# The output product of two chunks as seven block products, formed with Strassen's scheme, in a one-core layer kernel

## The chip, the cores and the metric

The kernel runs on one core of a Trainium2 chip. The metric is the device time of one execution in microseconds (us). The engines are TensorE (PE in the profile, its weight loads PEld), VectorE (DVE), ScalarE (ACT), GpSimd (POOL) and SyncE (SP), which here issues every DMA. Each has its own instruction stream and executes it in order; semaphores join them.

## What is computed

The reference, cut to the part that matters here (one layer, 2048 tokens, 1024 channels, float32):

```python
shift, scale, gate = jnp.split(jax.nn.silu(c) @ w_ada + b_ada, 3, axis=-1)
h = _layer_norm(x) * (1 + scale[:, None]) + shift[:, None]
xa, ga, u, v, gb = jnp.split(h @ w_in, SPLITS, axis=-1)          # 5 x 512 channels
ya = _pool_mixer(xa, w_pool, pool_scale) * jax.nn.silu(ga)
yb = _sgu_mixer(gelu(u), gelu(v), ...) * jax.nn.silu(gb)
y = jnp.concatenate([ya, yb], axis=-1) @ w_out                   # (2048,1024) @ (1024,1024)
z = DEEPNORM_ALPHA * x + gate[:, None] * y
return _layer_norm(z) * ln_g + ln_b
```

## The kernel before

The 2048 tokens are worked in four chunks of T = 512. Every product runs three times in float32r: both factors are split into a high part (ScalarE rounds, `wH`, `hH`, `yH`) and a low part (VectorE subtracts, `wL`, `hL`, `yL`), and `product` (L1050) issues high by high, high by low and low by high.

A chunk consists of units, each with one 128x1024 block of weights (512 KB). Units 0 to 3 (`V_UNITS`) make v in banks A, token by token. Units 4 to 19 are the channel units, four for each of the groups g = 0..3 (xa, ga, u, gb), in banks B 0 to 3. Units 20 to 27 are the output units: four make the first 512 columns of y @ w_out in banks A, four the second in banks B. A unit is 24 matmuls of 512 columns. Chunk 0 has a start of its own, chunks 1 and 2 are a loop (`run_chunks`, L230), and chunk 3 has its own end (`last_products`).

Weights pass through two float slots, `wF`. SP loads unit n+4 in its iteration n (`load_w`, L305) once the low part of unit n+2 is made; ScalarE copies unit n+2 in its iteration n (`split_high`, L511) into one of four slots once unit n-2 is done on TensorE; VectorE makes the low part (`split_low`, L658). The order of each engine's work within an iteration is written out by hand; tables say in which iteration a piece stands.

Pieces beside the units: `pooling`, `gate` and `y_pool` make the pooling branch of a group in `yP`, `sgu_sum`, `mix` and a multiplication by the gate the other branch in `mixed`; `y_low` makes the low parts. The next chunk's x is prepared meanwhile: statistics by tokens in iterations 10, 11, 14, 15 (`X_STATS_IN`); in iteration 16 SP sends means and reciprocal deviations through DRAM and loads x by channels; `x_normalise` (two VectorE instructions of 512 columns for each of eight rows) stands in iterations 19 to 22 (`X_CENTRE_IN`); `h_evacuate` on ScalarE and `h_split` on VectorE in 20 to 23.

After an output half, `z_half` (L892) multiplies the bank by the gate, adds it to ALPHA * x in `z` and takes statistics; the second half's are made in iterations 0 to 3 of the next chunk, with `z_norm` behind them. GpSimd makes the reciprocal deviations (`rstd`, L459: a power on one or four elements) in the order in which its stream holds them: z of the last chunk, v, x of the next. TensorE may start a chunk's v units when z's first-half products have read banks A.

## Time and profile before

| | |
|---|---|
| time, median of 3 | 673.99 us (673.91 to 674.61) |
| profiled execution | 673.68 us |
| its span, first to last instruction | 671.6 us |
| busy: TensorE, VectorE, ScalarE, GpSimd | 659.8, 516.1, 235.1, 61.7 us |
| mean granted TensorE clock | 0.998 of full speed |
| moved by DMA | 108.73 MB, 162 GB/s |

Busy times are sums over instructions; those of TensorE overlap each other, so a row's mean is longer than the distance from one matmul to the next. The chain is followed back from the last instruction and shows which engine set the end. Idle time in front of an instruction is written behind it with what ended it.

### The profile page before, as it was taken

The page shows a single profiled execution, that of the slowest core. Times are in us where ns is not written, and L with a number is a line of the kernel's source. Part 1 is how long each engine was busy: PE and PEld are TensorE (multiplying, and loading weights), DVE is VectorE, ACT ScalarE, POOL GpSimd, SP SyncE. Part 2 cuts the span into 40 slices and gives each one's busy share as a digit, 9 for nine tenths or more (in the row PEclk, how much of TensorE's full clock was granted, in tenths as well). Part 3 has the DMA queues.
Part 4 walks back from the last instruction along what each step waited for, and adds up shares of the span by engine and source line. Part 5 has one row for each costly group of instructions (what it writes and reads, how often), then busy time and mean ns, then how long its engine had stood idle before and what let it go on. Part 6 is the DMA issues. An engine that isn't in the chain of part 4 may idle for free.

```text
span 671.6 us, 8845 instructions
## 1 busy us (share of the span) xinstructions
PE 659.8 (98%) x3103; PEld 551.3 (82%) x3103; DVE 516.1 (77%) x956; ACT 235.1 (35%) x307; POOL 61.7 (9%) x77
## 2 busy tenths in 40 slices
PE   8999999999999999999999999999999999999995
PEld 8888888877888888888888888888888888888884
DVE  5678898749969967766979968775977986656776
ACT  4424644316522333224722332322821333323300
POOL 2000110100002201100002201000002210000010
PEclk9999999999999999999999999999999999999999
DMA  8995643785334472288243562378343454224111
GB/s 340 365 332 233 219 153 116 163 228 189 125 111 141 126 258 86 95 116 322 96 156 100 180 248 65 106 94 332 102 148 90 162 205 159 104 79 154 52 63 62
DMA packets 34546, 108.73 MB, mean 162 GB/s; under 512 B 6573, under 2 KB 7633, under 8 KB 34514
## 3 DMA queue, kind: packets, MB, share of 16 engines
q1 hardware_dynamic: 34514, 108.31, 49.5%
q8 instruction: 19, 0.31, 0.2%
q14 instruction: 13, 0.11, 0.1%
HBM read 97.80 MB, written 10.50 MB: 161 GB/s over the span
## 4 chain that ended last, share of the span: by engine, by line
PE 95%; issue 2%; DVE 2%; ACT 0%; DMA 0%; POOLq 0%; POOL 0%; DVEq 0%
PE bank_b L1053 63%; PE bank_a L1053 25%; PE bank_a L1180 2%; PE bank_a L1140 1%; PE bank_b L1113 1%; PE bank_a L1171 1%; DVE w_low L656 1%; PE bank_b L1077 0%; DVE v_gelu L708 0%; PE bank_b L1171 0%; PE bank_b L1132 0%; PE bank_b L1104 0%; DMA vector_rows<-in_vectors 0%; ACT h_high L528 0%; ACT w_high L509 0%
## 5 line engine op out<-in xcount | busy, mean ns | idle before, releaser
L1053 PE MATMUL bank_b<-h_high,w_high 128*128 128x512 f32 x512 | 202.2, 395 | 0.2 <-DVE h_low L668 0.2
L1053 PE MATMUL bank_b<-h_low,w_high 128*128 128x512 f32 x512 | 199.3, 389 | 0.0
L1053 PE MATMUL bank_b<-h_high,w_low 128*128 128x512 f32 x512 | 199.3, 389 | 0.0
L661 DVE TENSOR_TENSOR w_low<-w_float,w_high 128x1024 fp32r<-128x1024 f32 x98 | 119.5, 1220 | 40.3 <-ACT w_high L518 40.2
L518 ACT ACTIVATE w_high<-w_float 128x1024 fp32r<-128x1024 f32 x98 | 103.4, 1056 | 130.5 <-DMA w_float<-in_w_units 57.2
L1053 PEld LDWEIGHTS bank_b<-h_high,w_high 128*128 128x128 f32 x512 | 96.2, 188 | 20.2 <-issue 1.1
L1053 PEld LDWEIGHTS bank_b<-h_high,w_low 128*128 128x128 f32 x512 | 96.1, 188 | 20.1
L1053 PEld LDWEIGHTS bank_b<-h_low,w_high 128*128 128x128 f32 x512 | 96.2, 188 | 19.5 <-issue 0.5
L461 POOL TENSOR_TENSOR z_rstd<-z_var_eps,minus_half 128x1 f32<-128x1 f32 x16 | 22.0, 1377 | 361.8 <-DVE z_var_eps L905 351.9
L1053 PE MATMUL bank_a<-w_high,y_high 128*128 128x512 f32 x128 | 49.9, 390 | 0.2 <-issue 0.2
L1053 PE MATMUL bank_a<-w_high,y_low 128*128 128x512 f32 x128 | 49.8, 389 | 0.0
L1053 PE MATMUL bank_a<-w_low,y_high 128*128 128x512 f32 x128 | 49.8, 389 | 0.0
L1053 PE MATMUL bank_b<-w_high,y_high 128*128 128x512 f32 x96 | 37.3, 389 | 0.0
L1053 PE MATMUL bank_b<-w_low,y_high 128*128 128x512 f32 x96 | 37.3, 389 | 0.0
L1053 PE MATMUL bank_b<-w_high,y_low 128*128 128x512 f32 x96 | 37.3, 389 | 0.0
L1053 PE MATMUL bank_a<-w_high,h_high 128*128 128x512 f32 x96 | 37.3, 389 | 0.0
L1053 PE MATMUL bank_a<-w_low,h_high 128*128 128x512 f32 x96 | 37.3, 389 | 0.0
L1053 PE MATMUL bank_a<-w_high,h_low 128*128 128x512 f32 x96 | 37.3, 389 | 0.0
L461 POOL TENSOR_TENSOR x_rstd<-x_var_eps,minus_half 128x1 f32<-128x1 f32 x16 | 20.1, 1255 | 138.8 <-DVE x_var_eps L684 138.8
L611 ACT ACTIVATE tanh<-bank_b 128x512 f32<-128x512 f32 x15 | 9.0, 598 | 60.8 <-PE bank_b L1053 60.8
L1053 PEld LDWEIGHTS bank_a<-w_high,y_high 128*128 128x128 f32 x128 | 24.0, 188 | 5.6 <-issue 0.6
L1053 PEld LDWEIGHTS bank_a<-w_high,y_low 128*128 128x128 f32 x128 | 24.0, 188 | 5.0
(180 smaller groups left out, 934.0 us busy)
## 6 DMA issues: line engine op xcount, KB each, us to landing
w_float<-in_w_units SPq DMA_DIRECT2D x90, 512.0 KB, 3.4
x_norm<-in_x SPq DMA_DIRECT2D x16, 512.0 KB, 4.5
z<-in_x SPq DMA_DIRECT2D x16, 512.0 KB, 5.2
out<-z SPq DMA_DIRECT2D x15, 512.0 KB, 4.8
z<-in_mod_units SPq DMA_DIRECT2D x12, 512.0 KB, 9.1
x_norm<-in_x_channels SPq DMA_DIRECT2D x12, 512.0 KB, 15.0
w_float<-xa_units SPq DMA_DIRECT2D x12, 512.0 KB, 3.5
mod_spare<-in_mod_units SPq DMA_DIRECT2D x6, 512.0 KB, 8.6
```

The source lines that it names most:

```text
L461: nc.gpsimd.tensor_tensor(rstd_out, var_eps, exponent, ALU.pow).then_inc(ready, 1)
L518: nc.scalar.activation(wH[:, n % S_SLOTS, :], w_float(c, n), ACT.Copy).then_inc(w_high, 1)
L611: nc.scalar.activation(tanh[:, :], B[:, 1, :], ACT.Tanh, scale=0.5).then_inc(ga_tanh, 1)
L656: vec.tensor_tensor(low, early_float(unit), high.bitcast(F32), ALU.subtract).then_inc(w_low, 1)
L661: vec.tensor_tensor(wL[:, n % S_SLOTS, :], w_float(c, n), wH[:, n % S_SLOTS, :].bitcast(F32), ALU.subtract).then_inc(w_low, 1)
L1053: last = mm(bank, wl if n == 2 else wh, ml if n == 1 else mh, start=start and n == 0, stop=stop and n == 2)
L1113: last = mm(B[:, 3, at:at + P], m_slot(m)[:, col:col + P], c_col.broadcast_to([P, P]), start=(m % 2 == 0 and a == 0 and s == 0), stop=(m = ...
L1140: mm(A[:, 0, 0:P], ident[:, :], ones[:, :], start=True, stop=True)
L1171: last = mm(banks[k // 4][:, k % 4 * P:(k % 4 + 1) * P], xa_float(g)[:, cut], wpF[:, g * P:(g + 1) * P], start=True, stop=True)
L1180: last = mm(A[:, 2 + h % 2, j * P:(j + 1) * P], gv[:, j, cut], wt[:, cut], start=True, stop=True)
```

## The change

Chunks 1 and 2 (`FAST`) make the output product as a 2 x 2 block product in the Winograd form of Strassen's scheme: y is cut by tokens (256 and 256) and by branch (pooling and SGU), the weights by branch and by output half. Seven block products take the place of eight; each is two units of 12 matmuls, so such a chunk has 14 output units. The gate is multiplied into the weights beforehand.

- In chunk 0, from the moment the gate is known, GpSimd forms the seven weight blocks for each quarter q of the input channels (`prepare_out_units`), SP loads the weights for it in iterations 18, 19, 24, 26 and stores the seven half-units (256 KB each) to DRAM in iterations 23, 25, 27 and in iteration 1 of chunk 1. Chunk 1's v activation waits for all of the stores, since the last tiles lie in `gv`.
- In the fast chunks GpSimd forms the sums of y for each group (`sums_of_y`); ScalarE and VectorE split two of them at once and two in iterations 25 to 28.
- VectorE adds each product's banks to z as it is finished (`add_parts`); products 4 to 6 reuse banks B.
- The preparation of the next x moves in the fast chunks: statistics to iterations 8 to 11, rows to 12, centring to 16 to 19, h to 22 to 32.
- The loop over chunks 1 and 2 is unrolled; unit counts go through `base(c)`.

The core of the diff:

```diff
+FAST = (1, 2)
+PRODUCTS = 7
+FAST_UNITS = IN_UNITS + 2 * PRODUCTS
+PARTS = ((0, 0, 0, 0), (0, 1, 1, 0), (1, 2, 2, 0), (1, 3, 3, 0), (2, 4, 0, 0), (2, 5, 1, 0), (3, 6, 2, 1), (3, 7, 3, 1),
+         (4, 4, 0, 1), (4, 5, 1, 1), (5, 6, 0, 1), (5, 7, 1, 1), (6, 4, 2, 1), (6, 4, 2, 0), (6, 5, 3, 1), (6, 5, 3, 0))
+READ_IN = {IN_UNITS + 3 + 2 * i: i for i in range(PRODUCTS - 1)}
+LATE_IN = {25: 0, 26: 1, 27: 2, 28: 3}
...
+FAST_X_STATS_IN = {8: 0, 9: 1, 10: 2, 11: 3}
+FAST_X_ROWS_IN = 12
+FAST_X_CENTRE_IN = {16: (0, 1), 17: (2, 3), 18: (4, 5), 19: (6, 7)}
+FAST_H_IN = {22: (0,), 23: (1,), 24: (2,), 26: (3,), 28: (4,), 29: (5,), 30: (6,), 32: (7,)}
...
-            chunk(0, True, False)
-            with eng.Fori(1, CHUNKS - 1) as c:
-                chunk(c, False, False)
-            chunk(CHUNKS - 1, False, True)
+        def run_chunks(chunk):
+            for c in range(CHUNKS):
+                chunk(c, c == 0, c == CHUNKS - 1)
...
+            def prep_load(q):
+                if q == 0:
+                    sp.wait_ge(w_low, XA_ALONE[-1] + 1)
+                elif q == 1:
+                    sp.wait_ge(sgu_done, G)
+                else:
+                    sp.wait_ge(out_stored, (q - 1) * PRODUCTS * 16)
+                for half in range(2):
+                    sp.dma_start(prep_tile(q, half), w_units[IN_UNITS + half * G + q]).then_inc(prep_landed[q % 2][half], 16)
+            def prep_store(q):
+                sp.wait_ge(prep_ready, q + 1)
+                zero, one = prep_tile(q, 0), prep_tile(q, 1)
+                for i, half_unit in enumerate((zero[:, 0:T], t4[:, :], zero[:, T:], t12[:, 0:T], t12[:, T:], one[:, 0:T],
+                                               one[:, T:])):
+                    cut = slice(q % 2 * T, (q % 2 + 1) * T)
+                    sp.dma_start(out_units[i, q // 2][:, cut], half_unit).then_inc(out_stored, 16)
...
+            def prepare_out_units():
+                gp = nc.gpsimd
+                pool.wait_ge(gate_ready, 2)
+                for q in range(G):
...
+                        pool.wait_ge(prep_landed[q % 2][half], (q // 2 + 1) * 16)
+                        done = gp.tensor_tensor(rows, rows, gate.broadcast_to([P, 2, T]), ALU.mult)
+                    prep_steps.then(pool, done)
+                    b21, b11, b22, b12 = zero[:, 0:T], zero[:, T:], one[:, 0:T], one[:, T:]
+                    wait(pool, out_stored, q * PRODUCTS * 16)
+                    prep_steps.then(pool, gp.tensor_tensor(t12[:, 0:T], b12, b11, ALU.subtract))
+                    prep_steps.then(pool, gp.tensor_tensor(t12[:, T:], b22, t12[:, 0:T], ALU.subtract))
+                    gp.tensor_tensor(t4[:, :], b21, t12[:, T:], ALU.subtract)
+                    gp.tensor_tensor(b12, b22, b12, ALU.subtract).then_inc(prep_ready, 1)
+            def sums_of_y(c, g):
...
+                gp.tensor_tensor(s12[:, 0:half], a21, a22, ALU.add).then_inc(s_steps, 1)
+                pool.wait_ge(s_steps, nth + 1)
+                gp.tensor_tensor(s12[:, half:], s12[:, 0:half], a11, ALU.subtract).then_inc(s12_ready, 1)
+                gp.tensor_tensor(s34[:, g, 0:half], a11, a21, ALU.subtract)
+                pool.wait_ge(s12_ready, nth + 1)
+                gp.tensor_tensor(s34[:, g, half:], a12, s12[:, half:], ALU.subtract).then_inc(s34_ready, 1)
...
+                        if n == ys_in[g] and c in FAST:
+                            act.wait_ge(ys_ready, c * G + g + 1)
+                            nc.scalar.activation(aH[:, g, :], mixed[:, 0:T // 2], ACT.Copy)
+                            act.wait_ge(s12_ready, FAST.index(c) * G + g + 1)
+                            nc.scalar.activation(yH[:, G + g, :], s12, ACT.Copy).then_inc(ys_high, 1)
...
+            def add_parts(c, i):
+                nth = FAST.index(c) * len(PARTS)
+                dve.wait_ge(unit_done, base(c) + IN_UNITS + 2 * i + 2)
+                for p, (product, bank, j, half) in enumerate(PARTS):
...
+                    if earlier:
+                        dve.wait_ge(part_read, nth + earlier[0] + 1)
+                        ins = vec.tensor_tensor(z[:, j, cut], psum, z[:, j, cut], ALU.add)
+                    else:
+                        dve.wait_ge(z_landed[j], (c + 1) * 16)
+                        ins = vec.scalar_tensor_tensor(out=z[:, j, cut], in0=z[:, j, cut], scalar=ALPHA, in1=psum,
+                                                       op0=ALU.mult, op1=ALU.add)
+                    ins.then_inc(part_read, 1)
...
+            def fast_unit(c, w, i, r):
...
+                if r == 0 and i >= 4:
+                    pe.wait_ge(part_read, nth * len(PARTS) + 2 * i - 2)
+                bank0 = (0, 2, 4, 6, 4, 6, 4)[i]
+                for qq in range(2):
+                    q = 2 * r + qq
+                    if i == 0:
+                        pe.wait_ge(yp_low, c * G + q + 1)
+                    if i == 2:
+                        pe.wait_ge(ys_low, c * G + q + 1)
+                    if i == 5:
+                        pe.wait_ge(s34_low, nth * G + q + 1)
...
+                    for t in range(2):
+                        psum = (A, B)[bank0 // 4][:, bank0 % 4 + t, :]
+                        cut = slice(col + t * P, col + (t + 1) * P)
+                        done = product(psum, high[:, at, cut], low[:, at, cut], w[0][:, block], w[1][:, block],
+                                       start=(i < 4 and q == 0), stop=(q == G - 1), skip_group_check=(i > 3))
```

## Rows read from the trace of the kernel before

**Rows 1.** the page: busy per engine, its slices of DMA, the chain

```profile
PE 659.8 (98%) x3103; PEld 551.3 (82%) x3103; DVE 516.1 (77%) x956; ACT 235.1 (35%) x307; POOL 61.7 (9%) x77
...
GB/s 340 365 332 233 219 153 116 163 228 189 125 111 141 126 258 86 95 116 322 96 156 100 180 248 65 106 94 332 102 148 90 162 205 159 104 79 154 52 63 62
...
PE 95%; issue 2%; DVE 2%; ACT 0%; DMA 0%; POOLq 0%; POOL 0%; DVEq 0%
```

**Rows 2.** the chain in order of time, chunk 2: start, us, what

```profile
464.05 21.76 PE bank_a L1053 x96
```

**Rows 3.** windows: chunk 0's output units; chunk 1's v units, channel units

```profile
core 0: us, PE busy (x) PEld busy (x) DVE busy (x) ACT busy (x) POOL busy (x), PEclk, DMA share, GB/s
151.90:195.70 43.80, 43.80 (x193) 36.27 (x194) 36.05 (x49) 21.86 (x27) 0.00 (x0) 1.00 0.44 150
195.70:217.40 21.70, 21.70 (x97) 17.96 (x97) 21.00 (x34) 4.25 (x4) 6.20 (x4) 1.00 0.37 122
217.40:308.10 90.70, 90.70 (x418) 75.68 (x417) 64.50 (x143) 28.98 (x40) 10.11 (x8) 1.00 0.53 153
```

**Rows 4.** groups by shape: busy us, mean ns; idle before

```profile
L661 DVE TENSOR_TENSOR w_low<-w_float,w_high 128x1024 fp32r<-128x1024 f32 x98 | 119.5, 1220 | 40.3 <-ACT w_high L518 40.2
...
L668 DVE TENSOR_TENSOR h_low<-sum_a,h_high 128x512 fp32r<-128x512 f32 x16 | 11.0, 687 | 2.2 <-ACT sum_a L529 2.2
...
L897 DVE TENSOR_TENSOR tanh<-bank_a,gate_rows 128x512 f32<-128x512 f32 x15 | 10.3, 684 | 0.3 <-PE bank_a L1053 0.3
...
L1030 DVE SCALAR_TENSOR_TENSOR z<-z,tanh 128x256 f32<-128x256 f32 x2 | 0.9, 426 | 0.1
```

**Rows 5.** chunk 2's float slots: VectorE, ScalarE, DMA to landing

```profile
484.02 1.22 DVE L661 TENSOR_TENSOR w_low<-w_float,w_high 128x1024 fp32r<-128x1024 f32 x1
...
488.57 1.06 ACT L518 ACTIVATE w_high<-w_float 128x1024 fp32r<-128x1024 f32 x1 [1.14 <-DMA w_float<-in_w_units]
...
DMA to landing us min/median/max: 3.2/3.3/3.3
```

**Rows 6.** VectorE in order of time, chunk 2's iterations 16 to 19

```profile
442.92 0.69 DVE L975 TENSOR_TENSOR mixed<-mixed,gate_b 128x512 f32<-128x512 f32 x1
...
447.58 0.18 DVE L821 COPY xa<-xa_halo 128x16 f32<-128x16 f32 x1 [1.11 <-ACT xa L608]
...
451.43 1.22 DVE L661 TENSOR_TENSOR w_low<-w_float,w_high 128x1024 fp32r<-128x1024 f32 x1
...
454.43 0.74 DVE L865 SCALAR_TENSOR_TENSOR mixed<-bank_a,half_cols,sgu_bias 128x512 f32<-128x512 f32 x1
461.25 1.23 DVE L661 TENSOR_TENSOR w_low<-w_float,w_high 128x1024 fp32r<-128x1024 f32 x1 [6.07 <-ACT w_high L518]
...
463.59 0.68 DVE L689 TENSOR_TENSOR x_norm<-x_norm,x_mean_rows 128x512 f32<-128x512 f32 x1
...
464.92 0.69 DVE L689 TENSOR_TENSOR x_norm<-x_norm,x_mean_rows 128x512 f32<-128x512 f32 x1
```

**Rows 7.** GpSimd's selections, by shape

```profile
L478 POOL TENSOR_SCALAR_AFFINE_SELECT y_pool<-y_pool 128x512 f32<-128x512 f32 x1 | 1.0, 962 | 25.2 <-DMA y_pool<-in_w_sgu 25.2
...
L456 POOL TENSOR_SCALAR_AFFINE_SELECT identity<-identity 128x128 f32<-128x128 f32 x1 | 0.3, 292 | 0.0
```

**Rows 8.** GpSimd's powers in order of time, and VectorE beside one

```profile
198.37 1.50 POOL L461 TENSOR_TENSOR z_rstd<-z_var_eps,minus_half 128x1 f32<-128x1 f32 x1 [70.19 <-DVE z_var_eps L905]
...
223.45 1.04 POOL L461 TENSOR_TENSOR v_rstd<-v_var_eps,minus_half 128x4 f32<-128x4 f32 x1 [0.41 <-DVE v_var_eps L883]
...
639.01 0.56 POOL L461 TENSOR_TENSOR z_rstd<-z_var_eps,minus_half 128x1 f32<-128x1 f32 x1 [95.25 <-DVE z_var_eps L905]
...
198.24 1.23 DVE L661 TENSOR_TENSOR w_low<-w_float,w_high 128x1024 fp32r<-128x1024 f32 x1
```

**Rows 9.** VectorE at the end of chunk 0's output units

```profile
187.07 0.68 DVE L897 TENSOR_TENSOR tanh<-bank_a,gate_rows 128x512 f32<-128x512 f32 x1
...
195.71 0.69 DVE L897 TENSOR_TENSOR tanh<-bank_b,gate_rows 128x512 f32<-128x512 f32 x1 [3.02 <-PE bank_b L1053]
```

More of the change, by code:

```diff
@@ L228, in wait, with units, base, own @@
                 eng.wait_ge(s, value)
-        def run_chunks(eng, chunk):
-            chunk(0, True, False)
-            with eng.Fori(1, CHUNKS - 1) as c:
-                chunk(c, False, False)
-            chunk(CHUNKS - 1, False, True)
+        def run_chunks(chunk):
+            for c in range(CHUNKS):
+                chunk(c, c == 0, c == CHUNKS - 1)
+        def units(c):
+            return FAST_UNITS if c in FAST else UNITS
+        def base(c):
+            return sum(units(i) for i in range(c))
+        def own(c, n):
+            return (c, n) if n < units(c) else (c + 1, n - units(c))
+        def classic(c):
+            return sum(1 for i in range(c) if i not in FAST)
         def places(first):
@@ L376, in chunk @@
             def chunk(c, first, last):
-                for n in range(V_UNITS if first else 0, UNITS):
+                _, x_rows_in, _, _ = x_tables(c)
+                for n in range(V_UNITS if first else 0, units(c)):
                     if first and n == V_UNITS + 2:
@@ L407, in chunk @@
                         sp.dma_start(xn[:, j, :], x_tiles[c + 1, j]).then_inc(xn_landed[j], 16)
-                    if not last and n == 16:
+                    if not last and n == x_rows_in:
                         sp.wait_ge(x_rstd, (c + 2) * TILES)
@@ L419, in chunk @@
                                 .then_inc(xT_landed[i], 16)
-                    if not last and n == 17:
+                    if not last and n == x_rows_in + 1:
                         sp.wait_ge(rows_stored, (c + 1) * 32)
@@ L491, in chunk @@
                     rstd(v_rstd, vve[:, j, :], vrs[:, j, :], minus_half[:, :])
-                if not last:
+                if c in FAST:
+                    x_rstds(c + 1, 0)
+                    x_rstds(c + 1, 1)
+                    sums_of_y(c, 0)
+                    x_rstds(c + 1, 2)
+                    x_rstds(c + 1, 3)
+                    for g in range(1, G):
+                        sums_of_y(c, g)
+                elif not last:
                     for j in range(TILES):
                         x_rstds(c + 1, j)
-            run_chunks(pool, chunk)
+                if first:
+                    prepare_out_units()
+            run_chunks(chunk)
             for j in range(TILES):
@@ L591, in chunk @@
                 sgu_after, mix_in, ys_in = places(first)
-                for n in range(FIRST_LOOP if first else 0, IN_UNITS + 1 if last else UNITS):
+                _, _, _, h_in = x_tables(c)
+                for n in range(FIRST_LOOP if first else 0, IN_UNITS + 1 if last else units(c)):
                     if not (last and n in LAST_SPLITS_IN):
@@ L639, in chunk @@
                                 .then_inc(gate_ready, 1)
-                    if not last and IN_UNITS <= n < IN_UNITS + 4:
-                        for k in range(2 * (n - IN_UNITS), 2 * (n - IN_UNITS) + 2):
+                    if not last and n in h_in:
+                        for k in h_in[n]:
                             h_evacuate(c + 1, k)
-            run_chunks(act, chunk)
+            run_chunks(chunk)
         @block.vector
@@ L858, in sgu_sum @@
                 wait(dve, ys_low, c * G + g)
+                done = sum(1 for i in FAST if i < c) * G + (g if c in FAST else 0)
+                wait(dve, s34_ready, done)
                 if first and g == 0:
@@ L941, in chunk @@
                     first_branches(c)
-                for n in range(FIRST_LOOP if first else 0, IN_UNITS + 1 if last else UNITS):
+                x_stats_in, _, x_centre_in, h_in = x_tables(c)
+                for n in range(FIRST_LOOP if first else 0, IN_UNITS + 1 if last else units(c)):
+                    if c in FAST and n in READ_IN:
+                        add_parts(c, READ_IN[n])
                     if not (last and n in LAST_SPLITS_IN):
```

221 lines of the change are left out of this document (166 added, 55 removed).

## The prediction

> **What bounds the kernel now.** I read the page first: TensorE is busy 98% of the span and makes 95% of the chain that ended last [rows 1]. The reader is to see there that only fewer matmuls, or a stall of TensorE, can move the end. The chain in order of time gives the price: 96 matmuls of 512 columns take 21.76 us wherever they stand [rows 2], so 0.2267 us each (the 389 ns of a single row overlap the next one and are no price). A unit of 24 is 5.44 us, the eight output units of a chunk 43.5 us. Then the windows by stage show what else is full: VectorE is busy 36.1 of 43.8 us in chunk 0's output stage and 21.0 of 21.7 us in the four v units after it; only the channel units leave it room, 64.5 of 90.7 us [rows 3]. GpSimd does nothing but small powers. So TensorE bounds, VectorE is second and close, and everything that the change gives VectorE, or puts in its way, has to be laid against that.
>
> **Matmuls removed.** A fast chunk has 14 units of 12 matmuls, 168, where there were 192. 48 fewer in two chunks are 48 x 0.2267 = 10.9 us, all on the path. The ideal output stage is 168 x 0.2267 = 38.1 us, and a fast unit 2.72 us. Nothing is regained if the same stage waits for 5.4 us.
>
> **Work added per fast chunk.** Six more units to split: ScalarE 1.06 us, VectorE 1.14 us each (a 1220 ns row, of which 0.08 overlaps the next start). Sixteen half-tile additions from PSUM to z at 0.61 to 0.72 us take the place of eight gate products and eight additions: even. Four late high/low pairs of 0.6 us, four half-size ones of about 0.4 us (256 columns take 426 ns) [rows 4].
>
> **The two float slots.** Each weight unit must land, be copied and be split before its slot is loaded again. In chunk 2 the split that began at 484.02 ended at 485.24, the load issued behind it took 3.3 us, ScalarE copied at 488.57, VectorE could split from 489.65 to 490.87 [rows 5]. The ring is 3.3 + 1.06 + 1.22 + 0.07 = 5.65 us for two units; TensorE now asks for two in 5.44, where before it asked for two in 10.9. A ring that was half idle becomes the pace.
>
> **VectorE into the output stage, in before's clock of chunk 2.** The eight centrings move from iterations 19 to 22 into 16 to 19; each is 1.33 us [rows 6]. I lay the work end to end from 443.6, where the third SGU group's gated product ends: wait for GpSimd's two sums and ScalarE's copy 2.0 (GpSimd priced below, 0.55 each; before, the wait was 0.7), the two low parts 1.0, centring 2.66, split 1.14, pooling of the last group 3.85, centring 2.66, split 1.14, gate, product and sum 2.28, centring 2.66, split 1.14, mix and low part 1.20, centring 2.66, split 1.14, gate and product 1.47, the GpSimd wait again 2.0, low parts 1.0, split 1.14. That is 31.1 us and ends at 474.7 with the split of unit 23. The 6.07 us that VectorE idled before 461.25 are used up. TensorE wants unit 23 at 464.05 + 3 x 2.72 = 472.2: a stall of 2.5 us. The statistics of x that leave iterations 14 and 15 go into earlier idle time and cost nothing: those iterations begin with waits for ScalarE. If the cover fails, 2 us each come on top.
>
> From there the ring gives unit 33 five turns later, 474.7 + 28.25 = 503.0, and the stage ends at 505.7: 41.6 us. But VectorE serves the ring in order. Fourteen splits are 16.0 us, twelve PSUM additions, each pair behind a finished product, 8.0, eight low parts of h and four late ones 7.3: 31 of the 38 us. Adding the ring's waits where they fall, unit 28 (its bank is free only after product 2 was added in iteration 27) starts 2.5 us late, and units 27, 30 and 32 lose 0.1 to 0.6 each; that lay-out ends at 508.9, 44.8 us. Bounds are 38.1 and 44.8; between 41.6 and 44.8 I take 43.0, because the waits of additions and of the ring partly coincide. So a fast stage gains 0.5 us instead of 5.4, two gain 1.0. The v units after it get less VectorE work (no gate product; the first takes four additions), so they cost nothing; TensorE's banks B are asked for 22 us later.
>
> **GpSimd's preparation in chunk 0.** Before has no large two-input GpSimd instruction. The nearest are the selections: 128x128 in 0.29 us and 128x512 in 0.96, a slope of 1.74 ns per element with one input [rows 7]. Two inputs cost no less, and at most double, 3.5 ns; I take a quarter above the row, 2.2, nearer to the row. Per quarter of the weights it does two products of 1024 and four differences of 512, 4096 elements: 9.0 us; four are 36 us (28.5 and 57 at the bounds); a sum of 256 columns in the fast chunks is 0.55 us.
>
> Can it lie beside VectorE? The power on a single element tells. It takes 0.56 us at 639.01, and 1.50 at 198.37, begun beside a 1024-column difference of VectorE that ran to 199.47; so do 25 of its 32 rows on one element, at 1.46 to 1.59 us, all but the first four and the last few [rows 8]. Four elements beside VectorE's work on v, which reads one tensor, take 1.04 us at 223.45. So GpSimd waits out VectorE's instructions with two SBUF inputs. That the reverse holds no row shows; but whichever yields, the two are not abreast, and someone waits for each: GpSimd's products are waited for by SP's in-order stores (behind which the weight loads stand) and its z powers by VectorE. So I price them as one resource.
>
> The Trainium skill (SBUF — State Buffer, Who interferes with whom) says that a VectorE instruction with two SBUF inputs and a GpSimd instruction that reads SBUF exclude each other for the whole instruction. The rows above agree for GpSimd's side. Its GPSIMD Engine Reference, Performance versus the Vector engine, gives 4497 ns for a 2048-element tensor_tensor, so 36.0 us for the preparation, which would leave the sum as it is.
>
> It starts near 154: the gate is in SBUF at 151.8, the first loads go out near 147 behind a full DMA stretch. Nearly all that VectorE does from there to 187 has two SBUF inputs, save the z products, statistics and one gate. Its last product on banks A ends at 187.8 while the v units need them at 195.7: 8 us of room [rows 9]. With the round trip of each store (1.8 MB, about 6 us at the 340 GB/s that the page's fullest slices show [rows 1]) GpSimd does about 22 of its 36 us by then. 5 us of it fall on other VectorE work, 2 into idle time: 15 us late against 8 of room, TensorE stalls 7. The last 14 us meet a VectorE that is 97% full in the v units; 5 us of idle before them and about 4 us of overlap leave some 5 more of lateness, most of it inside the two-unit lead of the splits: 1 us. Sum 8 us; at 1.74 ns 3 to 4 us. At 3.5 ns it is 8 + 21 = 29 us. Below nothing it can't go, as nothing is taken out. ScalarE's v activation waits for the last store: done near 212, needed at 217.4; free, but a late GpSimd would show there.
>
> DMA: 4.2 MB loaded and 7.3 MB stored over some 65 us, 177 GB/s on 120 to 150 [rows 3]; each store holds a weight load up by some 5.5 us, but before the fast chunks the ring has 10.9 us a turn. Free there. Unrolling removes loop branches that the chain doesn't show: 0. Fewer matmuls, no change of the granted clock, 1.00 throughout.
>
> **Sum.** The terms come from the profiled execution, 673.68 us for a span of 671.6; the median of the runs is 0.3 us above it, 673.99. 673.7 - 1.0 + 8 = 680.7, and with the 0.3 us 681.0 us.
>
> **Rivals.** (a) *Preparation hidden, fast stage at the ring's pace.* GpSimd and VectorE run side by side, or the waiting falls on GpSimd alone in gaps. For it: only 1-element reads are seen to collide. Then stages of 40.6 to 41.6 us: 674.0 - 2 x 2.4 = 669.2. It decides for faster once the preparation costs under about 4 us with stages under 41.6. Chance 0.25. (b) *Preparation hidden, stage 43.0*: 673.0. Chance 0.15. (c) *Two inputs double GpSimd's element*: 674.0 - 1.0 + 29 = 702; 0.10. (d) *Full gain*: neither ring nor VectorE shows, 663 to 666; against it the ring row. 0.04. My forecast, 676 to 688, has 0.46.
>
> A measurement tells 0.2%, 1.3 us, from nothing. Faster: 0.25 of (a), 0.05 of (b), 0.04 of (d), 0.03 from the forecast's edge, 0.37. Same 0.08, mostly (b). Slower 0.55. The range 667 to 690 takes in (a), (b), the forecast and the lower bounds; it leaves (c) and (d), 0.14, outside, and the forecast's far edge.
>
> **What would show it.** In the profile after: 48 fewer 512-column matmuls in fast chunks; GpSimd's products near 2.3 us alone and longer beside splits; VectorE's splits in chunk 0's output stage above 1.22 us, or late; TensorE idle just before chunk 1's first v unit; in the fast chunks, output stages near 43 us with ScalarE's copies waiting for loads, and gaps ahead of units 23 and 28. I'm wrong if VectorE's rows keep 0.69 and 1.22 us beside GpSimd's large ones, or if the fast stages take under 41 us.

## The result, and the profile after

The changed kernel takes 715.18 us, median of four executions (714.60 to 717.07), beside 673.95 us for the kernel before on the same chip: a ratio of 1.0617, 95% interval 1.0594 to 1.0641. That is 41 us slower, where 7 us slower was forecast and 690 us was the top of the range.

The page of the changed kernel: busy times of two engines, granted TensorE clock by slices, the chain. It answers to [rows 1].

```profile
PE 666.6 (93%) x3055; PEld 548.3 (77%) x3055; DVE 555.0 (78%) x984; ACT 254.4 (36%) x335; POOL 128.3 (18%) x133
...
PEclk9999999998999999999899999999899999999998
...
PE 37%; DVE 30%; DMA 13%; issue 9%; POOL 5%; ACT 4%; SPq 1%; POOLq 0%; DVEq 0%; ACTq 0%
```

TensorE has its 48 matmuls fewer (3055 for 3103), yet its busy time is longer, and the chain, 95% TensorE before, is TensorE for 37% only, with VectorE, DMA and GpSimd for 48%. VectorE's busy time rose by 39 us, though it has only 28 more instructions (12 of them are splits of weights, `w_low`, of 1.22 us). Windows by stage, for [rows 3]: chunk 0's output units, chunk 1's v, channel and output units, chunk 2's output units.

```profile
152.10:207.46 55.36, 45.50 (x193) 36.93 (x193) 47.09 (x47) 20.79 (x26) 29.28 (x14) 0.94 0.60 217
207.46:230.91 23.45, 22.02 (x97) 17.92 (x97) 15.62 (x20) 4.25 (x4) 18.44 (x12) 1.00 0.73 262
230.91:333.74 102.83, 94.39 (x416) 76.28 (x416) 80.12 (x168) 30.78 (x44) 21.59 (x22) 0.98 0.54 159
333.74:385.96 52.22, 44.39 (x168) 34.12 (x169) 42.77 (x55) 29.59 (x38) 2.85 (x4) 0.90 0.53 176
498.89:551.13 52.24, 43.08 (x168) 33.27 (x169) 42.64 (x55) 29.99 (x38) 2.85 (x4) 0.93 0.54 177
```

The first column after the window is the stage's length. Against before (43.8, 21.7, 90.7 and 43.5 us) the first three grew by 11.6, 1.7 and 12.1 us, and each fast output stage by 8.7 us. There are two separate losses: one from chunk 0's output units on, where GpSimd prepares the weights, and one in each fast stage.

**The first loss.** VectorE in order of time, in chunk 0's output units:

```profile
154.45 2.76 DVE L839 TENSOR_TENSOR x_norm<-x_norm,x_rstd_rows 128x512 f32<-128x512 f32 x1
157.14 3.42 DVE L810 TENSOR_TENSOR w_low<-w_float,w_high 128x1024 fp32r<-128x1024 f32 x1
160.48 0.68 DVE L993 SCALAR_TENSOR_TENSOR gate_b<-tanh,bank_b 128x512 f32<-128x512 f32 x1
...
170.19 2.71 DVE L839 TENSOR_TENSOR x_norm<-x_norm,x_rstd_rows 128x512 f32<-128x512 f32 x1
...
174.03 1.21 DVE L810 TENSOR_TENSOR w_low<-w_float,w_high 128x1024 fp32r<-128x1024 f32 x1
```

and GpSimd beside it, with the row after its long wait:

```profile
154.16 5.31 POOL L582 TENSOR_TENSOR mod_spare<-mod_spare,gate_rows 128x1024 f32<-128x1024 f32 x2 [25.69 <-DMA mod_spare<-in_w_units]
159.55 2.15 POOL L586 TENSOR_TENSOR w_spare<-mod_spare 128x512 f32<-128x512 f32 x1
...
166.76 5.58 POOL L582 TENSOR_TENSOR v_gelu<-v_gelu,gate_rows 128x1024 f32<-128x1024 f32 x2
194.19 1.29 POOL L586 TENSOR_TENSOR w_spare<-v_gelu 128x512 f32<-128x512 f32 x1 [21.84 <-DMA out_units<-mod_spare]
...
200.97 4.71 POOL L582 TENSOR_TENSOR mod_spare<-mod_spare,gate_rows 128x1024 f32<-128x1024 f32 x2
```

A normalisation of 0.69 us takes 2.76 us, a split of 1.22 us takes 3.42 us. The pair of GpSimd products ends at 159.47 and the split 1.09 us later: it stands still until the product is done and then takes about its own time. The row at 160.48 reads one tensor from a bank and keeps its 0.68 us beside a GpSimd difference. As GpSimd stops at 172.3, the split is back at 1.21 us. GpSimd itself takes 1.29 us for a difference of 512 when it is alone and 2.15 us beside VectorE. The split at 174.03 is unit 23's. In the kernel before the same split is this row:

```profile
162.62 1.22 DVE L661 TENSOR_TENSOR w_low<-w_float,w_high 128x1024 fp32r<-128x1024 f32 x1
```

There it ended 4.4 us ahead of TensorE's need (at 162.62 + 1.22, needed at 151.90 + 3 x 5.44). In the changed kernel TensorE stands from 168.70 for it, 6.59 us, and this is what the granted clock does (windows of 2 us, PEclk is the third number from the end):

```profile
166.00:168.00 2.00, 2.00 (x10) 1.65 (x10) 2.00 (x2) 0.69 (x1) 2.00 (x2) 1.00 0.00 0
...
172.00:174.00 2.00, 0.00 (x0) 0.00 (x0) 2.00 (x3) 0.38 (x1) 0.35 (x1) 0.50 0.00 0
174.00:176.00 2.00, 0.71 (x2) 0.61 (x3) 1.97 (x4) 2.00 (x4) 0.00 (x0) 0.50 0.00 0
176.00:178.00 2.00, 2.00 (x6) 1.54 (x5) 1.97 (x4) 1.49 (x2) 0.00 (x0) 0.50 0.80 260
178.00:180.00 2.00, 2.00 (x10) 1.63 (x9) 2.00 (x3) 1.39 (x2) 0.00 (x0) 0.94 0.02 6
```

In the stall it falls from 1.00 to 0.50 (from 2.4 to 1.2 GHz) and it is back only after some 3 us of work, in which the same matmuls take twice as long: 6 of them between 176 and 178, 10 in a window at full clock.

SP in order of time: it comes to the first store at 185.63, to the last group of stores at 226.60, and the weight load that is queued behind those goes out at 230.88. So ScalarE, in the second fence, starts a copy for the channel units late:

```profile
185.63 0.43 SPq L400 DMA_DIRECT2D out_units<-mod_spare  x1
...
226.60 0.32 SPq L400 DMA_DIRECT2D out_units<-v_gelu  x1
...
230.88 0.33 SPq L375 DMA_DIRECT2D w_float<-in_w_units  x1
```

```profile
237.23 1.06 ACT L652 ACTIVATE w_high<-w_float 128x1024 fp32r<-128x1024 f32 x1 [11.40 <-DMA w_float<-in_w_units]
```

VectorE waits for GpSimd directly as well. The powers of z stand in GpSimd's stream behind the last quarter of the weights, so VectorE idles 5.15 us for them, and the split that follows at 229.63 is the one for which TensorE waits 1.43 us at the start of the channel units:

```profile
226.53 1.07 POOL L547 TENSOR_TENSOR z_rstd<-z_var_eps,minus_half 128x1 f32<-128x1 f32 x2
```

```profile
227.11 1.28 DVE L1099 SCALAR_TENSOR_TENSOR z<-z,z_mean_var,ln_g_rows 128x1024 f32<-128x1024 f32 x1 [5.15 <-POOL z_rstd L547]
```

**The second loss.** VectorE ahead of and in chunk 2's output stage, which begins at 498.89:

```profile
477.78 1.23 DVE L810 TENSOR_TENSOR w_low<-w_float,w_high 128x1024 fp32r<-128x1024 f32 x1 [9.23 <-ACT w_high L652]
...
482.83 0.69 DVE L1177 TENSOR_TENSOR mixed<-mixed,gate_b 128x512 f32<-128x512 f32 x1
485.84 0.98 DVE L1031 TENSOR_TENSOR ys_low<-mixed,ys_high 128x256 fp32r<-128x256 f32 x1 [2.32 <-ACT y_high L768]
...
503.63 1.22 DVE L810 TENSOR_TENSOR w_low<-w_float,w_high 128x1024 fp32r<-128x1024 f32 x1
...
508.62 1.22 DVE L810 TENSOR_TENSOR w_low<-w_float,w_high 128x1024 fp32r<-128x1024 f32 x1
...
515.05 2.35 DVE L810 TENSOR_TENSOR w_low<-w_float,w_high 128x1024 fp32r<-128x1024 f32 x2
```

The splits at 503.63, 508.62 and 515.05 are those of units 21, 22 and 23. TensorE waits for the first and the third, and later for a bank that `add_parts` reads (unit 28):

```profile
504.90 0.50 PE L1257 MATMUL bank_a<-w_high,y_high 128*128 128x512 f32 x1 [2.96 <-DVE w_low L810]
...
516.31 0.79 PE L1257 MATMUL bank_a<-w_high,y_high 128*128 128x512 f32 x1 [3.41 <-DVE w_low L810]
...
533.80 0.47 PE L1257 MATMUL bank_b<-w_high,y_high 128*128 128x512 f32 x1 [1.89 <-DVE z L1051]
```

With one of 0.52 us these gaps are 8.8 us. The stage is 52.24 us and its matmuls are 38.1. Of the other 5.3 us some 3.3 are matmuls at half clock, behind the two long gaps (TensorE's busy time times what the granted clock lacks of 1.00, summed over 50 windows of the stage); the rest is in gaps below 0.4 us and in the start behind each gap, where the first two matmuls stand 0.34 us apart and not 0.23.

The 9.23 us ahead of 477.78 are a wait for a weight load that SP issued behind the four loads of the next x by channels. It was issued at 462.80, and ScalarE copied its weights at 476.68:

```profile
457.75 1.93 SPq L504 DMA_DIRECT2D x_norm<-in_x_channels  x4
462.80 0.33 SPq L375 DMA_DIRECT2D w_float<-in_w_units  x1
```

The kernel before has the same pair four iterations later, and its 6.07 us ahead of 461.25 [rows 6] are the wait for it:

```profile
442.37 2.02 SPq L418 DMA_DIRECT2D x_norm<-in_x_channels  x4
446.51 0.34 SPq L316 DMA_DIRECT2D w_float<-in_w_units  x1
```

### The profile page after: what moved, and what is told of

The parts are those of the page before. It is cut to its first block, busy times and chain, and to the rows that moved or that the text cites. A ratio compares the mean times of both kernels' runs of the same rounds, so it can differ in the third digit from the quotient of the medians.

```text
span 715.3 us, 8443 instructions
## 1 busy us (share of the span) xinstructions
PE 666.6 (93%) x3055; PEld 548.3 (77%) x3055; DVE 555.0 (78%) x984; ACT 254.4 (36%) x335; POOL 128.3 (18%) x133
## 3 DMA queue, kind: packets, MB, share of 16 engines
q1 hardware_dynamic: 41426, 126.14, 53.7%
## 4 chain that ended last, share of the span: by engine, by line
PE 37%; DVE 30%; DMA 13%; issue 9%; POOL 5%; ACT 4%; SPq 1%; POOLq 0%; DVEq 0%; ACTq 0%
PE bank_b L1257 24%; DMA w_float<-in_w_units 8%; PE bank_a L1257 8%; DVE w_low L810 7%; DMA w_float<-out_units 3%; DVE x_norm L837 3%; DVE z L1101 1%; ACT w_high L652 1%; DVE z L1099 1%; SPq L400 1%; DVE x_stats L830 1%; DVE y_low L1033 1%; PE bank_a L1344 1%; DMA out_units<-mod_spare 1%; DVE mixed L1177 1%
## 5 line engine op out<-in xcount | busy, mean ns | idle before, releaser
L810 DVE TENSOR_TENSOR w_low<-w_float,w_high 128x1024 fp32r<-128x1024 f32 x110 | 139.6, 1271 | 58.3 <-ACT w_high L652 58.2
L652 ACT ACTIVATE w_high<-w_float 128x1024 fp32r<-128x1024 f32 x110 | 115.9, 1056 | 184.8 <-DMA w_float<-in_w_units 131.2
L1257 PEld LDWEIGHTS bank_b<-h_high,w_high 128*128 128x128 f32 x512 | 96.5, 189 | 31.1 <-DVE w_low L810 11.0
L1257 PEld LDWEIGHTS bank_b<-h_high,w_low 128*128 128x128 f32 x512 | 96.5, 189 | 20.3
L1257 PE MATMUL bank_a<-w_high,y_high 128*128 128x512 f32 x96 | 42.1, 438 | 21.3 <-DVE w_low L810 21.1
L547 POOL TENSOR_TENSOR z_rstd<-z_var_eps,minus_half 128x1 f32<-128x1 f32 x16 | 19.8, 1239 | 234.7 <-DVE z_var_eps L1094 117.2
L1257 PEld LDWEIGHTS bank_a<-w_high,y_high 128*128 128x128 f32 x96 | 19.8, 206 | 30.1 <-DVE w_low L810 25.5
L1257 PE MATMUL bank_a<-w_low,y_high 128*128 128x512 f32 x96 | 40.9, 426 | 0.0
L1257 PE MATMUL bank_a<-w_high,y_low 128*128 128x512 f32 x96 | 40.8, 425 | 0.0
L547 POOL TENSOR_TENSOR v_rstd<-v_var_eps,minus_half 128x4 f32<-128x4 f32 x16 | 16.4, 1024 | 78.8 <-DVE v_var_eps L1072 78.8
L1257 PEld LDWEIGHTS bank_b<-w_high,y_high 128*128 128x128 f32 x96 | 18.0, 188 | 10.3 <-issue 6.7
```

The lines of the kernel that those rows point to most:

```text
L547: nc.gpsimd.tensor_tensor(rstd_out, var_eps, exponent, ALU.pow).then_inc(ready, 1)
L652: nc.scalar.activation(w_of(c, n)[0], w_float(c, n), ACT.Copy).then_inc(w_high, 1)
L810: vec.tensor_tensor(low, w_float(c, n), high.bitcast(F32), ALU.subtract).then_inc(w_low, 1)
L1257: last = mm(bank, wl if n == 2 else wh, ml if n == 1 else mh, start=start and n == 0, stop=stop and n == 2, skip_group_check=skip_group_check)
```

## The experiments

Each ran beside the kernel before, which was at 673.2 to 674.0 us. The stages are the lengths of the output units of chunks 0, 1 and 2 and, in the middle, of chunk 1's channel units, in the profiled execution.

| kernel | median us | ratio, interval | out 0 | channel 1 | out 1 | out 2 |
|---|---|---|---|---|---|---|
| the change | 715.18 | 1.0617 (1.0594 to 1.0641) | 55.4 | 102.8 | 52.2 | 52.2 |
| no preparation | 692.98 | 1.0295 (1.026 to 1.033) | 43.5 | 92.8 | 51.8 | 51.9 |
| its DMAs alone | 697.23 | 1.0347 (1.0318 to 1.0376) | 43.7 | 96.5 | 52.0 | 52.1 |
| before + GpSimd work, two inputs | 700.65 | 1.0403 (1.0379 to 1.0426) | 70.7 | | | |
| before + GpSimd work, one input | 675.00 | 1.0013 (1.0003 to 1.0022) | 44.7 | | | |
| no preparation, x later | 689.60 | 1.0243 (1.022 to 1.0266) | | 90.7 | 51.1 | 51.4 |
| no preparation, loads of x spread | 683.83 | 1.0157 (1.0143 to 1.0171) | 43.6 | 90.7 | 49.3 | 49.1 |
| no preparation, matmuls as filler | 697.36 | 1.0356 (1.0338 to 1.0373) | | 92.1 | 53.7 | 53.8 |
| no preparation, no centring | 678.13 | 1.0064 (1.0047 to 1.008) | | | 46.5 | 45.6 |
| no preparation, small loads | 687.32 | 1.0196 (1.0176 to 1.0216) | | 93.0 | 49.3 | 50.4 |
| no preparation, short sums | 684.70 | 1.0151 (1.0125 to 1.0177) | | 90.7 | 48.8 | 50.7 |
| no centring, short sums | 668.83 | 0.9929 (0.9911 to 0.9947) | 43.6 | 90.7 | 40.5 | 40.2 |
| and small loads | 662.70 | 0.9835 (0.9818 to 0.9853) | 43.5 | 90.7 | 38.3 | 38.3 |

### Which of the two losses is the preparation's

**No preparation.** The output units load the old weight blocks, and nothing is loaded, computed or stored for the new ones.

```diff
-                if first:
-                    prepare_out_units()
...
-                    source = out_units[(n - IN_UNITS) // 2, (n - IN_UNITS) % 2]
+                    source = w_units[IN_UNITS + (n - IN_UNITS) % OUT_UNITS]
```

> The changed kernel without the preparation: no loads, GpSimd products and differences or stores of the seven weight blocks; the fast units load the old output units in turn, so the weights lack the gate and the block sums and the output is not the reference's. Theory A (two separate costs; the preparation's is all in chunk 0 and chunk 1 up to its output stage): the stages there return to the times of before, 25.5 us less than the changed kernel's 715, so 690, and the two output stages stay at 52 us each. Rival B (the fast stages are slow because the preparation's lateness is handed on): the output stages fall toward 43 us and the time to 672.

**Its DMAs alone.** All loads, stores and waits stay; GpSimd writes four single elements in place of the arithmetic.

```diff
+                    nc.gpsimd.memset(pool_spare[:, q:q + 1], 0.0).then_inc(prep_ready, 1)
-                    done = gp.tensor_tensor(rows, rows, gate.broadcast_to([P, 2, T]), ALU.mult)
...
```

> The changed kernel with the preparation's loads, stores and waits, but with one small GpSimd memset in place of each quarter's two products and four differences (the stored blocks are then not sums, the output is not the reference's). Theory A (VectorE and GpSimd exclude each other while both read SBUF): the stall of 6.6 us at 168.7 and the low clock behind it go, VectorE's splits are 1.22 us again, and chunk 0's output stage falls from 55.4 to 48 or less; the stores still hold the weight loads up. About 703. Rival B (transfers alone make the loss): no more than 3 us less than 715.

The preparation costs 22.2 us (715.18 less 692.98) and the fast stages keep 51.8 and 51.9 us without it, so the losses are separate. Of the 22.2 the DMAs with their waits are 4.3 us (697.23 less 692.98), known to about 3 us, as the runs without preparation lie between 691.0 and 695.4. The arithmetic is 18.0, with what waits in a queue behind it (the stores, the powers of z); the runs don't part these.

**GpSimd's arithmetic on the kernel before, and the same with one input.** The first adds the preparation's 24 instructions on free tiles to the kernel before, with no DMA, and only GpSimd's own later powers queued behind them; the second multiplies by a constant in each.

```diff
+            chunk(0, True, False)
+            pool_work()
...
-                        done = gp.tensor_tensor(rows, rows, gate.broadcast_to([P, 2, T]), ALU.mult)
+                        done = gp.tensor_scalar(tile, tile, 0.5, None, ALU.mult)
...
-                    pool_work_steps.then(pool, gp.tensor_tensor(t[:, 0:T], b12, b11, ALU.subtract))
+                    pool_work_steps.then(pool, gp.tensor_scalar(t[:, 0:T], b12, 0.5, None, ALU.mult))
```

> The kernel before with the preparation's arithmetic added on GpSimd in the same place (eight products of 1024 columns and sixteen differences of 512, on tiles that are free there), without any load or store and without anyone waiting for its result except the in-order powers of z behind it. Theory A (exclusion): VectorE loses about as much as GpSimd works, 40 us less what falls in gaps, in a stretch where it has 8 us of room: the time rises by 10 to 20 us. Rival B (they share without loss): within 1 us of 674. Rival C (the exclusion only delays GpSimd): VectorE's rows keep 0.69 and 1.22 us.

> The kernel before with GpSimd multiplying free tiles by a constant, in the place, the number and the sizes of the preparation's instructions (per quarter two of 1024 columns and four of 512), so that each of them reads one tensor from SBUF and not two. The kernel before with the two-input instructions took 700.7 us, 27 us above before. Theory A (what holds VectorE up is GpSimd reading two tensors): VectorE's splits keep 1.22 us beside them, 674 to 678 us. Rival B (any large GpSimd instruction excludes VectorE's two-input ones, reading one or two): splits of 2.5 to 3.5 us and 685 to 697 us, less than 700.7 by the shorter element alone.

Two inputs cost 27 us, more than the 10 to 20 that were expected, and one input 1.0. VectorE in the kernel with two inputs:

```profile
176.73 2.83 DVE L691 TENSOR_TENSOR h_low<-sum_b,h_high 128x512 fp32r<-128x512 f32 x1
179.49 3.37 DVE L684 TENSOR_TENSOR w_low<-w_float,w_high 128x1024 fp32r<-128x1024 f32 x1
182.78 1.76 DVE L712 TENSOR_TENSOR x_norm<-x_norm,x_mean_rows 128x512 f32<-128x512 f32 x1
```

and in the kernel with one:

```profile
164.94 1.52 DVE L689 TENSOR_TENSOR h_low<-sum_b,h_high 128x512 fp32r<-128x512 f32 x1
166.38 1.21 DVE L682 TENSOR_TENSOR w_low<-w_float,w_high 128x1024 fp32r<-128x1024 f32 x1
167.51 0.68 DVE L710 TENSOR_TENSOR x_norm<-x_norm,x_mean_rows 128x512 f32<-128x512 f32 x1
```

```profile
158.44 1.49 POOL L506 TENSOR_SCALAR w_spare<-mod_spare 128x512 f32<-128x512 f32 x1
...
164.83 6.00 POOL L503 TENSOR_SCALAR mod_spare<-mod_spare 128x1024 f32<-128x1024 f32 x2
```

The one-input instructions are not shorter (1.49 us for 512 columns, 1.29 with two inputs alone), and GpSimd is busy 46.3 of the 48 us from 152 to 200. Of VectorE's 42 splits and 512-column rows with two SBUF inputs beside them 27 keep their length; the other 15 are stretched by 8.0 us in sum, one split to 2.05 us. With two inputs on GpSimd's side all 24 are stretched, by 32.2 us. So one input disturbs VectorE as well, by a quarter as much, and the splits' lead takes most of it: TensorE's gaps are two of under 1 us. In both kernels TensorE's gaps are waits for splits, of 14.29 and 6.76 us with two inputs, and no split waits for GpSimd by a semaphore. So what costs 27 us is VectorE held up by GpSimd's two-input instructions; it needs neither a queue nor a store. The edit changed the kind of the instruction (`tensor_scalar` for `tensor_tensor`) together with the number of its inputs; which of the two matters isn't shown.

### What makes a fast stage 52 us

**x later** (rows in iteration 16, centring in 19 to 22), on the kernel without preparation:

```diff
-FAST_X_ROWS_IN = 12
-FAST_X_CENTRE_IN = {16: (0, 1), 17: (2, 3), 18: (4, 5), 19: (6, 7)}
+FAST_X_ROWS_IN = 16
+FAST_X_CENTRE_IN = {19: (0, 1), 20: (2, 3), 21: (4, 5), 22: (6, 7)}
```

> As no_prep (no preparation, the output is not the reference's), and the fast chunks' rows are sent in iteration 16 and x is centred in iterations 19 to 22, as in the kernel before; the statistics stay in 8 to 11. Theory A (VectorE enters the output stage late because 8 us of centring stand in iterations 16 to 18): VectorE comes to unit 20's split on time, but has 41 us of work in a stage of 38: the output stages take 44 to 47 us and the time is 5 to 12 us under no_prep. Rival B (the ring of two float slots is the pace): the output stages stay within 1 us of no_prep's.

Theory A missed: the stages only went to 51.1 and 51.4 us, within the 1 us of rival B. That doesn't make the ring the pace, as the runs below show; another wait took the place of the first. The third group's product came 20.3 us ahead of the stage again, as before the change, but VectorE's wait for the loads of x came back behind it, and the centring lay in the first fast units:

```profile
468.26 1.23 DVE L796 TENSOR_TENSOR w_low<-w_float,w_high 128x1024 fp32r<-128x1024 f32 x1 [5.41 <-ACT w_high L640]
```

**Loads of x spread.** The same bunch of loads, issued one in each of iterations 12 to 15, and the centring where the change has it.

```diff
-                    for i in range(TILES):
+                    if not last and x_rows_in <= n < x_rows_in + TILES:
+                        for i in [n - x_rows_in] if c in FAST else range(TILES) if n == x_rows_in else []:
```

> The changed kernel without the preparation (its output is wrong, as the weights of the output product are the old ones), and in chunks 1 and 2 SP issues the four loads of the next x by channels one in each of the iterations 12 to 15, where it issued all four in iteration 12. With them bunched a weight load of chunk 2 issued behind them took over 10 us, VectorE idled 7.94 us for it before 451.61, and the third group's gated product ended at 457.35, 16.5 us ahead of the output stage at 473.88, where the prediction had counted 20.4 us. Theory A (that idle time is a cause of the late units 21 to 23): the idle time falls to under 3 us, the product ends 19 to 21 us ahead of the stage, unit 23 starts some 4 us earlier than 16.3 us into the stage, the stages take 47 to 50 us in place of 51.8 and 51.9; 684 to 690 us. Rival B (the load only moves the wait, and VectorE is late by its own work all the same): the stages stay within 1 us of 51.8 and 51.9; 691 to 694 us.

9.2 us come back (692.98 less 683.83), 2.1 of them in chunk 1's channel units. The idle time of 7.94 us ahead of the third group fell to 2.67, and the next split, which had none, waits 2.56 us, so 2.7 us of VectorE's time are won there:

```profile
442.37 1.23 DVE L797 TENSOR_TENSOR w_low<-w_float,w_high 128x1024 fp32r<-128x1024 f32 x1 [2.67 <-ACT w_high L641]
...
448.14 1.23 DVE L797 TENSOR_TENSOR w_low<-w_float,w_high 128x1024 fp32r<-128x1024 f32 x1 [2.56 <-ACT w_high L641]
...
450.07 0.69 DVE L1162 TENSOR_TENSOR mixed<-mixed,gate_b 128x512 f32<-128x512 f32 x1
```

The product ends 19.2 us ahead of the stage (469.93) and unit 23 starts 13.6 us into it, where it was 16.3: 2.7 us earlier for the 4 expected. The stages are in theory A's range, and rival B is out.

**Three causes, one at a time and together.** No centring: `x_normalise` on one column in chunks 1 and 2. Short sums: GpSimd's sums of y on one column. Small loads: output units 20 to 33 load 256 of 1024 columns. All three leave computation out.

```diff
+                cut = slice(0, 1) if c - 1 in FAST else slice(0, T)
-                vec.tensor_tensor(xT[:, k, :], xT[:, k, :], meanB, ALU.subtract).then_inc(x_centred, 1)
+                vec.tensor_tensor(xT[:, k, cut], xT[:, k, cut], meanB[:, cut], ALU.subtract).then_inc(x_centred, 1)
```

```diff
-                gp.tensor_tensor(s12[:, 0:half], a21, a22, ALU.add).then_inc(s_steps, 1)
+                gp.tensor_tensor(s12[:, one], a21[:, one], a22[:, one], ALU.add).then_inc(s_steps, 1)
```

```diff
+                cut = slice(0, 256) if c in FAST and n >= IN_UNITS else slice(0, 1024)
-                sp.dma_start(wF[:, n % F_SLOTS, :], source).then_inc(w_landed[n % F_SLOTS], 16)
+                sp.dma_start(wF[:, n % F_SLOTS, cut], source[:, cut]).then_inc(w_landed[n % F_SLOTS], 16)
```

> As no_prep, and in the fast chunks x_normalise works on one column of 512 (the next chunks' x is then not normalised; the output is not the reference's): 16 VectorE instructions of 0.69 us become 0.06, 10 us less of VectorE work ahead of each fast output stage. Theory A (VectorE is behind its work when the short units begin, and what TensorE loses there is waits plus low clock): the output stages of 51.8 and 51.9 us fall to 39 to 43, the clock stays at its upper level, and the time is near 693 - 20 = 673. Rival B (the ring of two float slots): the stages stay above 48.

> As no_prep, and the fast output units load only 256 of their 1024 columns (the rest of the float slot keeps what it held; the output is not the reference's), so the landing takes some 2.2 us in place of 3.3 and the ring 4.6 us in place of 5.65 for two units. Theory A (VectorE's order sets the pace): a stage gains at most 1.5 us, the time is 690 to 693. Rival B (the ring sets the pace): the stages fall to 45 or less and the time to 679.

> As no_prep, and GpSimd's sums of y work on one column (the blocks are then not sums; the output is not the reference's), so VectorE's wait of 2.33 us for GpSimd and ScalarE in each group shrinks by about 1.2 us and nothing of GpSimd lies beside its half-size low part. Theory A: two groups' waits fall in the critical stretch, so units 21 to 24 come 3 to 4 us earlier and one fall of the clock may go: 2 to 5 us per stage, time 683 to 689. Rival B (the sums are hidden): 693.

> The changed kernel without the preparation, and with both the centring of the next x and GpSimd's sums of y on one column in chunks 1 and 2 (both left out, so x of chunks 2 and 3 and y of 1 and 2 are wrong). The two float slots are as in the change. Theory A (VectorE's load, GpSimd's sums and the ring each hold the same iterations up, and VectorE's load stands for the most): the output stages of chunks 1 and 2 take 43 to 45 us (46.5 and 45.6 with the centring alone off), the ring's own pace of 5.65 us per two units (41.6) and unit 28's wait remain; 671 to 674 us. Rival B (what is left at 46 us has another cause, say TensorE's order or the additions from PSUM): no more than 0.7 us per stage below 46.5 and 45.6, 676 to 678 us.

> As the one above, and output units 20 to 33 of chunks 1 and 2 load 256 of 1024 columns, so that the float slots hold nothing up. Theory A: the three causes together are all, the stages come within 2 us of the 38.1 us of their matmuls: 38.5 to 40 us each, 664 to 667 us. Rival B (the additions from PSUM and unit 28's bank are a cause of their own): 41 to 44 us each with a gap ahead of unit 28 of 1.5 to 3 us, 669 to 674 us.

Singly centring, small loads and short sums give back 14.9, 5.7 and 8.3 us, together 28.8; centring and sums together give 24.2 (singly 23.1), all three 30.3. So they add up: none hides another. Short sums came as expected. Centring alone gave less than theory A said (stages of 46.5 and 45.6 us, not 39 to 43), and small loads alone lie between the theories (687.3, where A had 690 to 693 and the ring 679), so the ring has a part of its own. The pair gave more than theory A expected (668.8, not 671 to 674), and with all three the stages are bare matmuls. The windows of the output stages of chunks 1 and 2 with all three off:

```profile
307.45:345.74 38.29, 38.29 (x169) 31.53 (x168) 33.42 (x43) 28.38 (x36) 0.67 (x4) 1.00 0.32 103
458.17:496.45 38.28, 38.28 (x169) 31.53 (x168) 33.41 (x42) 28.26 (x36) 0.67 (x4) 1.00 0.31 104
```

The sixteen additions from PSUM, the late pairs and the wait for the bank of unit 28 are all still there and cost nothing. The wait was a consequence: it fell to 0.68 and 0.62 us with the pair off, and no gap of 0.3 us is left in these stages with all three.

**Matmuls as filler.** Ten small matmuls of an identity ahead of units 21, 22, 24 and 28 are to keep TensorE at work while it waits.

```diff
+                        for _ in range(10):
+                            mm((B if n < 28 else A)[:, 0, 0:P], ident[:, :], ones[:, :], start=True, stop=True)
```

> As no_prep (output not the reference's for that reason), and TensorE does ten 128-column float32 products of the identity into a free bank ahead of units 21, 22, 24 and 28 of the fast chunks, where it otherwise stands still for 1.8 to 2.0 us each; ten take about 1.7 us. Nothing else changes. Theory A (each wait costs a second time, because the granted clock falls to its lower level for 3 to 4 us behind it): the clock stays up and a stage is 4 to 5 us shorter, the time 683 to 686. Rival B (what is lost beyond the waits has another cause, such as the weight loads): the time stays at 693 or rises by up to 4.

This missed too; it is slower by 4.4 us. Windows of chunk 2's output stage in that kernel:

```profile
485.00:489.00 4.00, 4.00 (x29) 3.71 (x28) 3.93 (x6) 0.00 (x0) 0.00 (x0) 1.00 0.62 246
...
492.00:495.00 3.00, 0.00 (x0) 0.00 (x0) 2.65 (x4) 3.00 (x5) 1.03 (x2) 1.00 0.17 70
495.00:498.00 3.00, 2.90 (x9) 2.29 (x10) 2.98 (x5) 0.62 (x1) 0.00 (x0) 0.67 0.69 194
```

The clock stayed at 1.00 ahead of units 21 and 22, and TensorE then waited 3.39 us at once for unit 23's split, with 0.67 behind it. The filler missed that place: in the kernel without preparation the waits of chunk 2 stand ahead of units 21, 22, 23 and 28 (2.0, 1.98, 1.79 and 1.9 us), and there is no filler ahead of 23 but one ahead of 24, where nothing is waited for. So this run doesn't test theory A where it counted. It shows that where VectorE sets the dates, a TensorE at full clock reaches the next wait sooner. The filler's own time and the clock can't be parted by this run, and what the clock alone costs stays open.

## Why the prediction was wrong

The direction was right and so were both places; the time was 34 us above the forecast and 25 us above the range. By its own steps:

- **48 matmuls, 10.9 us, 38.1 us for a fast stage:** right. 3055 matmuls, and 38.29 us once nothing holds them up.
- **GpSimd's own time, 36 us:** nearly right. With pairs of products at 4.71 us and differences at 1.29 us, the shortest rows, four quarters are 39.5 us (4 x (4.71 + 4 x 1.29)), a tenth above.
- **The two engines as one resource:** right, and the reverse direction, which no row before showed, is shown now: VectorE's rows stretch beside GpSimd's. The Trainium skill (SBUF — State Buffer, Who interferes with whom) has a VectorE instruction with two SBUF inputs contend with any GpSimd instruction that reads SBUF. The run with two inputs agrees, 27 us and every such row stretched. The run with one input agrees only in part, as GpSimd reads SBUF there too and 27 of 42 rows kept their length, for 1.0 us. Rival (a) rested on the opposite and fell.
- **8 us for the preparation:** this step failed; it cost 22.2. The lateness was set against the room of VectorE's last product on banks A, 8 us at the end of the stage. TensorE asks much earlier: unit 23's split had 4.4 us of lead, GpSimd ran 18 us without a pause from 154.2, and the work of 7.2 us that VectorE does from 154.4 took 18.4. This first stall alone was 6.6 us, where the forecast had 7 for the whole stage. The stage lost 11.6 us: this stall, about 1.5 us of half clock behind it, and 3.27 us ahead of chunk 1's first v unit, where the forecast had looked for the stall; there the clock stayed at 1.00. The 5 us of lateness that the forecast left for later, at a price of 1 us, did not stay inside the splits' lead; the channel units lost 10.0 us (102.8 for 92.8).
- **"Free there" of the DMAs:** wrong by 4.3 us. The stores in SP's order held weight loads up, and SP's arrival at the first store, 185.6, left GpSimd idle for 21.8 us in between, which put its second half behind VectorE's work on z and v.
- **A fast stage of 43.0 us:** wrong by 9.2 us, and it splits at unit 23. *Ahead of it* 6.8 us: it started 17.4 us into the stage, laid out for 10.65. The chain of VectorE's work was right, 32.7 us for 31.1 (both GpSimd waits are 2.32 and 2.33 us for 2.0, the low parts beside its sums 0.98 us). Its start was not: the product ended 15.4 us ahead of the stage, not 20.4. "The 6.07 us that VectorE idled before 461.25 are used up" took a wait for spare time. It was the wait for a weight load behind the four loads of x by channels, and these moved with the rows to iteration 12; the idle time moved with them, to 9.23 us ahead of the product. Spreading the loads gave 9.2 us of kernel time back. With them spread unit 23 was still 3 us later than laid out (13.6), 1.3 by the product's lead (19.2 for 20.4) and 1.7 by the chain (32.8 for 31.1). *Behind it* 2.5 us: the stage went on for 34.8 us, 32.35 were taken, and the lay-out with the ring's waits in order, which was called a bound, has 34.15. So the 1.8 us taken off because the waits "partly coincide" were wrong. That 34.15 comes so near is luck in part: TensorE waited 1.9 us ahead of unit 28 for 2.5 laid out and 0.5 ahead of unit 32, and some 1.6 us are half clock behind the stall of unit 23, which the lay-out doesn't have.
- **"No change of the granted clock":** wrong. The mean is 0.978 for 0.998, and TensorE's busy time rose although it has fewer matmuls. How much of the 41 us is the clock's is not settled.
- **The range** took stalls as additions to a full-speed TensorE; rival (c), 702 us, put the high end on GpSimd's element, which was not what was off.

## What to carry to other kernels

Set a delay against the lead of the first consumer behind it, not against the room at a stage's end, and add to a stall what the matmuls behind it may lose at half clock (here 1.5 to 1.7 us behind most, nothing behind some). Before idle time is counted as room, look at what ended it: a wait for a DMA moves with the DMA. And a VectorE busy for 82 and 97% of two stages before [rows 3] leaves little room for a TensorE with less to do: of the eleven microseconds of matmuls, five could be had with the centring and the y sums out of VectorE's way (668.83 us) and all eleven only with small loads too (662.70 us). These runs leave work out; none had the gain with the whole computation.

## What the runs showed of the hardware

- A GpSimd instruction with two SBUF inputs and a VectorE one with two SBUF inputs run one after the other, either way round (VectorE 2.76 us for 0.69 and 3.42 for 1.22; GpSimd 2.15 for 1.29). With one input on GpSimd's side VectorE's rows lost 8.0 us in place of 32.2, and the kernel 1.0 us in place of 27.
- On GpSimd an instruction with one input was no shorter: 512 columns took 1.29 us with two inputs (`tensor_tensor`) and 1.49 with one (`tensor_scalar`, beside VectorE); 256 columns 0.74 us, for 0.55 estimated.
- TensorE's clock fell to its lower level behind stalls and stayed there for about 3 to 4 us of its next work: behind 6.59 us in chunk 0's output stage, behind 2.96 and 3.41 us in chunk 2's of the changed kernel. It did not fall each time, and the length of the gap doesn't tell when: it was 1.00 behind 1.60, 1.98 and 2.46 us of the kernel with spread loads, and in the changed one behind 1.89 us ahead of unit 28 and behind 3.27 us ahead of chunk 1's v units. In chunk 1's output stage of the changed kernel, with four gaps of 1.8 to 2.0 us, it was 0.5 behind the first, the third and the fourth. In the kernel without preparation it was 0.5 behind 1.89 us ahead of that stage, with no gap of 0.2 us in the 80 us before it. The kernel before has no gap of 0.4 us from 140 us to its last stage, and 1.00 there.
